# Half of the expert gates added up in a DRAM table by 128 indexed transfers, the other half still by one-hot products

## The chip, the cores and the metric

One core of one Trainium2 chip. The metric is device time in microseconds (us) of the whole program. The engines are TensorE (PE, matrix products), VectorE (DVE), ScalarE (ACT), GpSimd (POOL) and SyncE (SP, which issues most transfers).

## The reference, cut to what matters

The program is a decoder trunk of two layers over 256 tokens of width 1024. Each layer has a mixer, a cross-attention and an expert stage (PEER), and the change is in the last one:

```python
sc = jnp.einsum('thpc,hpkc->thpk', q, sub_keys)       # 8 heads, 2 sides, 128 keys
sv, si = lax.top_k(sc, TOPK)                          # 16 best keys of each side
cand = (sv[..., 0, :, None] + sv[..., 1, None, :])    # 256 sums
fv, fi = lax.top_k(cand, TOPK)                        # 16 best sums
eid = jnp.take_along_axis(cid, fi, axis=-1)           # expert = row key * 128 + column key
g = jax.nn.softmax(fv, axis=-1)
a = jax.nn.gelu(jnp.einsum('thkd,td->thk', ue, xb))
return jnp.einsum('thk,thkd->td', g * a, ve)
```

So each token chooses 16 experts of 16384 in each of 8 heads. The kernel does not gather them. It multiplies all 128 slabs of `u_experts` (a slab is 128 experts by 1024) with all tokens, takes the gelu, multiplies by a dense table of gates that is zero wherever a token has not chosen an expert, and multiplies the result with all 128 slabs of `v_experts`. An expert that a token has chosen in several heads gets the sum of its gates.

## The kernel before

**Slabs.** Weights come as slabs of 512 KB through a ring of `RING` = 4 buffers `raw`. A slab is loaded by SP (`next_slab`, as soon as its buffer is free), ScalarE rounds it to `w_hi` when TensorE has finished the slab that was in the same place (`half_of`, L721 to L725), VectorE makes `w_lo` as the rest (`lo_part`, L848), and TensorE multiplies with `w_hi` and `w_lo`. VectorE's `lo_part` is also what frees the `raw` buffer for the load of the slab four further on.

**The U stage** has 128 slabs. `wide_product` does a slab as 8 pairs of products (L1332 with 512 columns, L1333 with 256). For each slab ScalarE copies half of the result to one of two `h_out` slots, VectorE adds the other half (L1102), ScalarE takes the gelu (L731), and SP stores it to `h_park` in DRAM (L371, 128 KB). `half_of` waits for the store of two slabs before, which frees its slot.

**The choice** lies on VectorE, beside slabs 4 to 71 of U. After the scores of both blocks of 128 tokens come 32 selections of 16 out of 128, 16 of 16 out of 88, and a decoding of the positions to row and column keys (`pick`, L1187 to L1195) for both blocks together. VectorE's order is written out by hand: each piece of the choice calls `spend` with an estimated duration, and for every `LO_EVERY` = 1.56 us spent `next_lo` puts in the `add_u` and `lo_part` of one slab. ScalarE computes the exponentials of both blocks in one instruction after slab `EXP_AT` (L753). Before slab `RET_AT` = 70 TensorE waits for `decoded` and transposes rows, columns and gates of both blocks, six products of 128 columns.

**The gate table** `gate` is [128 columns, 128 rows, 256 tokens] in SBUF, 128 KB in each partition. It is built beside the slabs `HOT_AT` = 72 to 123: for each group of 4 tokens VectorE makes one-hot matrices (`hot_rows`), TensorE does 8 products of 128 columns (`gates_of`, L1690), and ScalarE copies the result (`gate_out`, L761). There are 64 groups, placed in pairs, one pair for every 13 of the chunks (eighths of a slab) by `GROUP_AT`. The slabs 124 to 127 follow without groups (L1326).

**The V stage**: SP loads `h_park` slab by slab, GpSimd multiplies it with `gate` (`gated`, L524), ScalarE and VectorE split it into high and low part (L781, L1253), and TensorE does 12 products of 512 columns (L1715). GpSimd has nothing to do in the U stage. Its list is a wait for `act_ready`, then for the last `hot_row_ready`, then a load of `par`, then the wait for `gate_copied`, then `gated`.

The temporaries of the choice lie in the memory of `gate`, all above 64 KB. `h_out` and the one-hot tiles lie in the memory of `xT`, which is stored to `x_park` before.

## Time and profile before

| | |
|---|---|
| Time, median of 3 runs | 2064.01 us (2063.68 to 2064.97) |
| Profiled execution | 2065.03 us, its span 2063.3 us |
| Granted TensorE clock | 0.999 |
| TensorE busy | 2042.0 us, 99% |
| VectorE, ScalarE, GpSimd busy | 1648.9, 1190.2 and 346.2 us |
| Moved by DMA | 435.54 MB, mean 211 GB/s |

The span is the time from the first to the last instruction of the profiled execution. Layer 0 runs from 0 to about 1020 us of it and layer 1 repeats it 1020.4 us later. In layer 0 the U stage begins at about 289 us and ends at 681 us, and the V stage ends at 1025 us.

### The profile page before, as it was taken

The numbers are of one execution on the slowest core, as the hardware profiler recorded it, in microseconds if no ns is written. First come the engines' busy times: TensorE is split into PE (matmuls) and PEld (weight loads), VectorE is DVE, ScalarE is ACT, GpSimd is POOL, SyncE is SP. The second block draws the span as 40 slices with busy tenths as digits, with TensorE's granted clock in tenths as the row PEclk, the third lists the DMA queues.
The fourth block names the chain that finished last, engine by engine and source line by source line (L and its number), as shares of the span: only waits on it lengthen the run. The fifth ranks groups of instructions, "written<-read, shape, count | busy, mean of one in ns | idle before, by whom it ended". The sixth has DMA issues, their size and how long they took to land.

```text
span 2063.3 us, 38390 instructions
## 1 busy us (share of the span) xinstructions
PE 2042.0 (99%) x11552; PEld 1757.6 (85%) x11552; DVE 1648.9 (80%) x3041; ACT 1190.2 (58%) x1901; POOL 346.2 (17%) x348
## 2 busy tenths in 40 slices
PE   8999999999999999999999999999999999999998
PEld 6888888888888888888888888888888898888886
DVE  7786769999998667676688858799999987676776
ACT  6545556667666555555565545566666665545554
POOL 4010110000000333333340101000000004333331
PEclk9999999999999999999999999999999999999999
DMA  6445457776656877777653554577665567777773
GB/s 222 149 161 169 162 201 236 235 232 209 205 193 199 266 243 240 262 241 241 209 191 127 187 178 164 193 235 239 219 222 196 197 218 255 241 241 262 240 240 126
DMA packets 174249, 435.54 MB, mean 211 GB/s; under 512 B 19504, under 2 KB 85040, under 8 KB 173136
## 3 DMA queue, kind: packets, MB, share of 16 engines
q1 hardware_dynamic: 173520, 430.06, 63.6%
q0 software_dynamic: 640, 4.32, 0.6%
q8 instruction: 53, 0.87, 0.2%
q14 instruction: 36, 0.29, 0.1%
HBM read 397.60 MB, written 36.70 MB: 210 GB/s over the span
## 4 chain that ended last, share of the span: by engine, by line
PE 90%; DVE 6%; ACT 2%; DMA 1%; issue 1%; POOL 0%; SPq 0%; ACTq 0%; DVEq 0%
PE ps L1715 33%; PE ps L1332 30%; PE ps L1333 15%; PE ps L1690 3%; DVE w_lo L848 2%; PE ps L1606 2%; PE ps L1326 2%; PE ps L1737 1%; ACT w_hi L725 1%; PE ps L1631 1%; PE ps L1665 1%; DMA h_park<-h_out 1%; PE ps L1588 1%; DVE pick L1187 1%; DMA raw<-slabs 0%
## 5 line engine op out<-in xcount | busy, mean ns | idle before, releaser
L848 DVE TENSOR_TENSOR w_lo<-raw,w_hi 128x1024 fp32r<-128x1024 f32 x674 | 836.3, 1241 | 264.1 <-ACT w_hi L793 189.5
L1332 PE MATMUL ps<-act,w_hi 128*128 128x512 f32 x2784 | 985.7, 397 | 0.0
L1333 PE MATMUL ps<-act,w_lo 128*128 128x256 f32 x2784 | 777.5, 279 | 0.0
L1332 PEld LDWEIGHTS ps<-act,w_hi 128*128 128x128 f32 x2784 | 521.7, 187 | 114.1 <-issue 0.4
L1715 PE MATMUL ps<-w_hi,act 128*128 128x512 f32 x1936 | 596.4, 389 | 0.0
L1333 PEld LDWEIGHTS ps<-act,w_lo 128*128 128x128 f32 x2784 | 525.5, 189 | 0.3
L793 ACT ACTIVATE w_hi<-raw 128x1024 fp32r<-128x1024 f32 x248 | 263.1, 1061 | 325.2 <-PE ps L1715 325.2
L1715 PEld LDWEIGHTS ps<-w_hi,act 128*128 128x128 f32 x1936 | 363.4, 188 | 75.7
L1715 PE MATMUL ps<-w_lo,act 128*128 128x512 f32 x968 | 376.6, 389 | 0.0
L524 POOL TENSOR_TENSOR h_in<-h_in,gate 128x256 f32<-128x256 f32 x250 | 242.5, 971 | 437.9 <-DMA h_in<-h_park 437.8
L725 ACT ACTIVATE w_hi<-raw 128x1024 fp32r<-128x1024 f32 x248 | 261.1, 1053 | 0.0
L1715 PEld LDWEIGHTS ps<-w_lo,act 128*128 128x128 f32 x968 | 181.7, 188 | 37.5
L552 ACT ACTIVATE w_hi<-raw 128x1024 fp32r<-128x1024 f32 x168 | 177.2, 1055 | 43.7 <-PE ps L1333 26.7
L1253 DVE TENSOR_TENSOR act<-h_in,act 128x256 fp32r<-128x256 f32 x250 | 192.3, 769 | 7.0 <-ACT act L781 7.0
L731 ACT ACTIVATE h_out<-h_out 128x256 f32<-128x256 f32 x248 | 103.3, 416 | 123.6 <-DVE h_out L1102 121.9
L721 ACT ACTIVATE h_out<-ps 128x256 f32<-128x256 f32 x248 | 94.6, 382 | 121.4 <-PE ps L1333 103.7
L516 POOL DMA_DIRECT2D par<-params x2 | 1.2, 593 | 784.5 <-DVE hot_row L1231 784.5
L1102 DVE TENSOR_TENSOR h_out<-h_out,ps 128x256 f32<-128x256 f32 x248 | 102.5, 413 | 16.0 <-ACT h_out L721 15.7
L781 ACT ACTIVATE act<-h_in 128x256 fp32r<-128x256 f32 x250 | 100.0, 400 | 10.1 <-POOL h_in L524 10.1
L1231 DVE TENSOR_TENSOR hot_row<-row_is,g_parts 128x512 f16<-128x512 f16 x256 | 96.7, 420 | 0.0
L1332 PE MATMUL ps<-pre,w_hi 128*128 128x512 f32 x224 | 79.6, 399 | 0.0
L761 ACT ACTIVATE gate<-ps 128x512 f32<-128x512 f32 x128 | 70.4, 591 | 6.1 <-PE ps L1690 6.1
(264 smaller groups left out, 1830.7 us busy)
## 6 DMA issues: line engine op xcount, KB each, us to landing
raw<-slabs SPq DMA_DIRECT2D x680, 512.0 KB, 4.2
h_park<-h_out SPq DMA_DIRECT2D x256, 128.0 KB, 2.3
h_in<-h_park SPq DMA_DIRECT2D x250, 128.0 KB, 3.9
memT<-mem POOLq DMA_DIRECT2D x2, 1024.0 KB, 7.7
skT<-sub_keys POOLq DMA_DIRECT2D x2, 1024.0 KB, 7.4
x_park<-xT SPq DMA_DIRECT2D x2, 1024.0 KB, 6.0
xT<-x_park SPq DMA_DIRECT2D x2, 1024.0 KB, 6.9
xT<-x SPq DMA_DIRECT2D x4, 256.0 KB, 6.2
```

Of the source, the lines that this page charges most:

```text
L524: nc.gpsimd.tensor_tensor(h[:, n:n + 1, :], h[:, n:n + 1, :], gate[:, ds(g * RING + j, 1), :], ALU.mult).then_inc(gated_ready, 1)
L552: nc.scalar.activation(w_hi[:, j].rearrange("p k c -> p (k c)"), raw[:, j, :], ACT.Copy).then_inc(hi_ready, 1)
L725: nc.scalar.activation(w_hi[:, j].rearrange("p k c -> p (k c)"), raw[:, j, :], ACT.Copy).then_inc(hi_ready, 1)
L731: nc.scalar.activation(slot, slot, ACT.Gelu).then_inc(act_evac, 1)
L781: nc.scalar.activation(hi[:, j:j + 1, :], h[:, j:j + 1, :], ACT.Copy).then_inc(ga_hi_ready, 1)
L793: nc.scalar.activation(w_hi[:, j].rearrange("p k c -> p (k c)"), raw[:, j, :], ACT.Copy).then_inc(hi_ready, 1)
L848: nc.vector.tensor_tensor(w_lo[:, j].rearrange("p k c -> p (k c)"), raw[:, j, :], w_hi[:, j].rearrange("p k c -> p (k c)").bitcast(FP32), ...
L1102: nc.vector.tensor_tensor(slot, slot, ps[:, n % RING:n % RING + 1, 0:T], ALU.add).then_inc(u_sum, 1)
L1253: nc.vector.tensor_tensor(lo[:, j:j + 1, :], h[:, j:j + 1, :], hi[:, j:j + 1, :].bitcast(FP32), ALU.subtract).then_inc(ga_ready, 1)
L1332: nc.tensor.matmul(ps[:, j, :], w_hi[:, j, k, :], a[:, :, k, :], start=(k == 0), stop=False)
L1333: return nc.tensor.matmul(ps[:, j, hi * T:hi * T + T], w_lo[:, j, k, :], a[:, hi, k, :], start=False, stop=(k == KB - 1))
L1715: last = nc.tensor.matmul(ps[:, 2 * b + half, :], a[:, j, b * P:(b + 1) * P], w[:, j, 4 * half:4 * half + 4, :].rearrange("p k c -> p (k c)"),
```

## The change

Tokens 0 to 127 (block 0) leave the one-hot way. A table `g_spread` of 8 MB in DRAM is laid out as [128 columns, 128 rows, 128 tokens]. In each layer GpSimd fills it with zeros by four transfers of 2 MB, waits for VectorE's `place_ready`, and issues 128 indexed transfers, one for each head and rank. Each adds 128 single values (one for each token) into the table at the places in `place_u`. After the 16 of a head it waits until all have landed. Then it loads the table back into `gate[:, 0]` by four transfers of 2 MB. Before the first `gated` it waits for them (`spread_back`).

The choice is done block by block: VectorE selects, decodes and normalises block 0 completely, then block 1. There are two exponentials, after slabs 32 and 68. The one-hot way serves tokens 128 to 255 only: 32 groups, in slabs 76 to 123, three transposes before slab 74. `gate` is now [128, 2, 128, 128], and the multiply in `gated` has a fourth dimension.

```diff
-GROUPS = T // 4
-HOT_AT = 72
-RET_AT = 70
-EXP_AT = 60
+GROUPS = P // 4
+HOT_AT = 76
+RET_AT = 74
+EXP_ATS = (32, 68)
...
 EARLY = RING - 1
 H_SLOTS = 2
 HOTS = 2
...
+        place_f = tmp("place_f", 0, [P, PH * TOPK])
+        place_u = tmp("place_u", 0.5, [P, PH * TOPK], U32)
+        g_flat = tmp("g_flat", 1, [P, PH * TOPK])
+        zeros = tmp("zeros", 40, [P, ZERO_ROWS, P])
+
+        g_spread = nc.dram_tensor("g_spread", (P * NKEYS * P, 1), FP32, kind="Internal").ap()
...
+            spread = g_spread.rearrange("(p n t) o -> p n (t o)", p=P, n=NKEYS)
...
+                nc.gpsimd.memset(zeros[:], 0.0).then_inc(zeros_set, 1)
+                pool.wait_ge(zeros_set, layer + 1)
+                for n in range(0, NKEYS, ZERO_ROWS):
+                    pool.dma_start(spread[:, n:n + ZERO_ROWS, :], zeros[:]).then_inc(zeroed, 16)
+                pool.wait_ge(zeroed, (layer + 1) * (NKEYS // ZERO_ROWS * 16))
+                pool.wait_ge(place_ready, layer * 2 + 2)
+                for h in range(PH):
+                    for i in range(h * TOPK, (h + 1) * TOPK):
+                        nc.gpsimd.indirect_dma_start(g_spread, bass.IndirectOffsetOnAxis(ap=place_u[:, i:i + 1], axis=0),
+                                                     g_flat[:, i:i + 1], None, compute_op=ALU.add).then_inc(scattered, 16)
+
+                    pool.wait_ge(scattered, (layer * PH + h + 1) * (TOPK * 16))
+                for n in range(0, NKEYS, ZERO_ROWS):
+                    pool.dma_start(gate[:, 0, n:n + ZERO_ROWS, :], spread[:, n:n + ZERO_ROWS, :]).then_inc(spread_back, 16)
+
                 pool.wait_ge(hot_row_ready, (layer + 1) * GROUPS + 1)
                 settle(pool)
                 pool.dma_start(par[:], params[ds(layer + 1, 1)].rearrange("o p f -> (o p) f")).then_inc(par_loaded, 16)
                 pool.wait_ge(gate_copied, (layer + 1) * GROUPS + RING)
                 settle(pool)
+                pool.wait_ge(spread_back, (layer + 1) * (NKEYS // ZERO_ROWS * 16))
+                settle(pool)
 
                 def gated(g, j, h, n):
 
                     pool.wait_ge(h_loaded[j], (layer * (V_SLABS // RING) + g) * 16 + 16)
                     settle(pool)
-                    nc.gpsimd.tensor_tensor(h[:, n:n + 1, :], h[:, n:n + 1, :], gate[:, ds(g * RING + j, 1), :],
+                    of_h = h[:, n, :].rearrange("p (b o t) -> p b o t", b=TB, o=1)
+                    nc.gpsimd.tensor_tensor(of_h, of_h, gate[:, :, ds(g * RING + j, 1), :],
                                             ALU.mult).then_inc(gated_ready, 1)
 
...
-                nc.scalar.activation(g_exp[:], g_exp[:], ACT.Exp).then_inc(gexp_ready, 1)
-                experts(EXP_AT, HOT_AT - RING - EXP_AT)
+                at = RING
+                for b, exp_at in enumerate(EXP_ATS):
+                    experts(at, exp_at - at)
+                    act.wait_ge(fin_ready, layer * TB + b + 1)
+                    chosen = g_exp[:, b * PH:(b + 1) * PH, :]
+                    nc.scalar.activation(chosen, chosen, ACT.Exp).then_inc(gexp_ready, 1)
+                    at = exp_at
+                experts(at, HOT_AT - RING - at)
...
-                    nc.scalar.activation(gate[:, :, 4 * n:4 * n + 4],
+                    nc.scalar.activation(gate[:, 1, :, 4 * n:4 * n + 4],
...
-                for n in range(0, TB * SETS, 2):
-                    if n % SETS == 0:
-                        dve.wait_ge(sc_evac, layer * TB + n // SETS + 1)
-                        settle(dve)
-                    src = (scores0, scores1)[n // SETS]
+                for b, src in enumerate((scores0, scores1)):
+                    dve.wait_ge(sc_evac, layer * TB + b + 1)
+                    settle(dve)
+                    for n in range(b * SETS, (b + 1) * SETS, 2):
+                        step.join()
+                        top16(*[(src[:, m % SETS, :], struck[:, m - n, 0:NKEYS], top_v[:, m, :], top_u[:, m, :])
+                                for m in (n, n + 1)], us=0.29)
                     step.join()
-                    top16(*[(src[:, m % SETS, :], struck[:, m - n, 0:NKEYS], top_v[:, m, :], top_u[:, m, :])
-                            for m in (n, n + 1)], us=0.29)
-                step.mark(nc.vector.tensor_copy(top_i[:], top_u[:]))
-
-                step.join()
-                for b in range(TB):
+                    step.mark(nc.vector.tensor_copy(top_i[:, b * SETS:(b + 1) * SETS, :], top_u[:, b * SETS:(b + 1) * SETS, :]))
...
+                    cs = slice(b * PH, (b + 1) * PH)
+                    flat = slice(b * PH * TOPK, (b + 1) * PH * TOPK)
+                    nc.vector.tensor_tensor(g_exp[:, cs], fin_v[:, cs], fin_v[:, cs, 0:1].to_broadcast([P, PH, TOPK]),
+                                            ALU.subtract).then_inc(fin_ready, 1)
+                    flat_i = fin_i[:, cs].rearrange("p c k -> p (c k)")
+                    step.mark(nc.vector.tensor_scalar(bit_u[:, flat], flat_i, 8, None, ALU.bitwise_and))
...
+                    spend(1.0)
...
+                        for a in range(TOPK):
+                            step.mark(nc.vector.scalar_tensor_tensor(
+                                pick[:, a, cs], place[:, flat].rearrange("p (c k) -> p c k", k=TOPK), float(a),
+                                keys[:, :, side, a].unsqueeze(2).to_broadcast([P, PH, TOPK]), ALU.is_equal, ALU.mult))
+                            spend(0.26)
+                        n = TOPK // 2
+                        while n:
+                            step.join()
+                            out = (found[:, flat].rearrange("p (o c k) -> p o c k", o=1, k=TOPK) if n == 1
+                                   else pick[:, 0:n, cs])
+                            step.mark(nc.vector.tensor_tensor(out, pick[:, 0:n, cs], pick[:, n:2 * n, cs], ALU.add))
+                            spend(0.07 * n + 0.2)
+                            n //= 2
+                    step.join()
+                    if b == 0:
+                        step.mark(nc.vector.scalar_tensor_tensor(place_f[:], col_f[:, flat], float(NKEYS), row_f[:, flat],
+                                                                 ALU.mult, ALU.add))
+                    dve.wait_ge(gexp_ready, layer * TB + b + 1)
+                    step.link(nc.vector.tensor_reduce(g_sum[:, cs], g_exp[:, cs], AX.X, ALU.add))
+                    step.link(nc.vector.reciprocal(g_sum[:, cs], g_sum[:, cs]))
+                    of_sum = g_sum[:, cs].unsqueeze(2).to_broadcast([P, PH, TOPK])
+                    if b == 0:
+                        dve.wait_ge(consts, 5)
+                        nc.vector.tensor_scalar(place_u[:], place_f[:], float(P), tok[:, 0:1], ALU.mult, ALU.add).then_inc(place_ready, 1)
+                        nc.vector.tensor_tensor(g_flat[:].rearrange("p (c k) -> p c k", k=TOPK), g_exp[:, cs], of_sum,
+                                                ALU.mult).then_inc(place_ready, 1)
+                    else:
+                        nc.vector.scalar_tensor_tensor(g_exp[:, cs], g_exp[:, cs], GATE_SCALE, of_sum,
+                                                       ALU.mult, ALU.mult).then_inc(decoded, 1)
                 while due[0] < HOT_AT + 1:
                     next_lo()
                 dve.wait_ge(ret_mm, layer + 1)
-                step.mark(nc.vector.tensor_copy(pick_at[:].rearrange("p i n e -> p (i n e)"), ps[:, 4, :]))
-                g_pairs = ps[:, 5, 0:T].rearrange("p (n e) -> p n e", e=2)
+                step.mark(nc.vector.tensor_copy(pick_at[:].rearrange("p i n e -> p (i n e)"), ps[:, 4, 0:T]))
+                g_pairs = ps[:, 4, T:T + P].rearrange("p (n e) -> p n e", e=2)
...
-                    for b in range(TB):
-                        last = nc.tensor.transpose(ps[:, 4 + i // 2, (i % 2) * T + b * P:(i % 2) * T + (b + 1) * P],
-                                                   src[:, b * P:(b + 1) * P], ident[:])
+                    last = nc.tensor.transpose(ps[:, 4, i * P:(i + 1) * P], src[:, P:2 * P], ident[:])
```

## Rows read from the trace of the kernel before

**Rows 1.** The page: busy time of each engine, its share and instructions.

```profile
PE 2042.0 (99%) x11552; PEld 1757.6 (85%) x11552; DVE 1648.9 (80%) x3041; ACT 1190.2 (58%) x1901; POOL 346.2 (17%) x348
```

**Rows 2.** Windows of layer 0: length, busy time of each engine, clock, DMA share, GB/s.

```profile
365.00:385.00 20.00, 20.00 (x117) 17.62 (x117) 19.39 (x70) 12.73 (x23) 0.00 (x0) 1.00 0.71 238
...
445.00:465.00 20.00, 20.00 (x117) 17.64 (x116) 17.99 (x34) 13.57 (x23) 0.00 (x0) 1.00 0.77 240
...
485.00:505.00 20.00, 19.75 (x136) 17.18 (x135) 18.66 (x40) 11.48 (x22) 0.00 (x0) 1.00 0.71 217
```

**Rows 3.** The chain in order of time: start, length, what.

```profile
197.28 1.75 PE ps L1619 x16
...
529.08 0.93 PE ps L1690 x16
534.58 0.93 PE ps L1690 x16
...
681.16 337.31 PE ps L1715 x1488
```

**Rows 4.** Timeline of TensorE, first and last of 48 wide products: start, length.

```profile
433.93 0.39 PE L1332 MATMUL ps<-act,w_hi 128*128 128x512 f32 x1
...
450.23 0.39 PE L1332 MATMUL ps<-act,w_hi 128*128 128x512 f32 x1
```

**Rows 5.** Timeline of VectorE in the first choice: one slab's two operations and what follows.

```profile
340.98 0.40 DVE L1102 TENSOR_TENSOR h_out<-h_out,ps 128x256 f32<-128x256 f32 x1
341.31 1.23 DVE L848 TENSOR_TENSOR w_lo<-raw,w_hi 128x1024 fp32r<-128x1024 f32 x1
342.45 0.48 DVE L1115 MAX8 top_v<-scores 128x8 f32<-128x128 f32 x2
```

**Rows 6.** Timeline of VectorE: end of the second choice, then three of the pick operations.

```profile
437.75 0.42 DVE L1161 TENSOR_TENSOR g_exp<-fin_v 128x256 f32<-128x256 f32 x1
...
445.63 1.09 DVE L1187 SCALAR_TENSOR_TENSOR pick<-a_at,top_i 128x256 bf16<-128x256 bf16 x3
446.63 0.41 DVE L1102 TENSOR_TENSOR h_out<-h_out,ps 128x256 f32<-128x256 f32 x1
```

**Rows 7.** Groups of instructions over the whole run.

```profile
L1124 DVE MAX8 top_v<-struck 128x8 f32<-128x128 f32 x64 | 15.4, 284 | 0.1
...
L1124 DVE MAX8 fin_v<-struck 128x8 f32<-128x88 f32 x32 | 6.4, 243 | 0.1
```

**Rows 8.** Timeline of ScalarE at the one exponential of a layer.

```profile
461.67 1.28 ACT L753 ACT_TABLE_LOAD   x1
...
463.40 1.28 ACT L721 ACT_TABLE_LOAD   x1
...
466.04 1.28 ACT L731 ACT_TABLE_LOAD   x1
```

**Rows 9.** Timeline of GpSimd at the start of the value stage.

```profile
665.45 0.59 POOL L516 DMA_DIRECT2D par<-params  x1 [392.23 <-DVE hot_row L1231]
672.37 3.41 POOL L524 TENSOR_TENSOR early_in<-early_in,gate 128x256 f32<-128x256 f32 x3 [6.33 <-DMA early_in<-h_park]
```

**Rows 10.** The page: DMA issues, KB each, us from issue to landing.

```profile
h_park<-h_out SPq DMA_DIRECT2D x256, 128.0 KB, 2.3
```

**Rows 11.** DMA queues (packets, MB, share) during GpSimd's memT load: 24-26, then 1047-1048 us.

```profile
q0 software_dynamic: 81, 0.66, 82.1%
q1 hardware_dynamic: 27, 0.11, 13.4%
...
q0 software_dynamic: 37, 0.30, 72.0%
q1 hardware_dynamic: 25, 0.10, 25.4%
```

**Rows 12.** DMA from 530 to 660 us: totals, then issues with us to landing.

```profile
DMA packets 11099, 25.60 MB, mean 197 GB/s; under 512 B 1231, under 2 KB 6095, under 8 KB 11087
...
raw<-slabs SPq DMA_DIRECT2D x38, 512.0 KB, 3.5
```

76 lines of the change are left out of this document (28 added, 48 removed).

## The prediction

> **What bounds the kernel now.** The page's busy times come first: TensorE is busy for 2042.0 of 2063.3 us, VectorE for 80% of the span [rows 1]. The windows of layer 0 then show whether that holds beside the work that is changed. In the choice TensorE has 20.00 of 20 us and VectorE 19.39. Only the window before the one-hot groups has a hole, of 0.25 us [rows 2]. The chain of waits in order of time runs through the groups of one-hot products in a steady beat of one pair every 5.50 us, and the V stage is one piece of 337 us [rows 3]. So the reader is to see that TensorE sets the time, that what leaves its list is gained in full, and that VectorE is close behind. GpSimd is free in the whole U stage, but its queue feeds the same DMA engines as SP's, which carry 197 GB/s there [rows 12].
>
> The sum is made against the profiled execution, 2065.03 us. That is 1.0 above the median of the three timed runs. Two per mille of the time, 4.1 us, is about what a measurement can tell from no change.
>
> **TensorE.** 48 wide products took 16.30 us from the first to the last start, 47 steps of 0.3468 [rows 4], so a slab takes 2.774 us. A pair of groups comes every 5.50 us with 13 chunks, 4.51 us, around it [rows 3]. The rest, 0.99 us, is the pair, 0.495 for a group. Its 16 products alone are 0.93, which is the lower bound (0.465). There are 32 groups fewer in each of two layers: 64 × 0.495 = 31.7 us (29.8 by the lower bound). Three transposes in a layer go too. 16 of the attention's took 1.75 us [rows 3], so six are 0.7 us. Together −32.4 us, for 2032.6 if nothing else moves. Slabs 72 to 75 only change from having groups beside them to having none.
>
> **VectorE.** One slab's two operations take 1.47 us of its list (340.98 to 342.45, [rows 5]). The four slabs more before HOT_AT bring 4 × 2.774 of time and take 4 × 1.47, so 5.2 us are added for the choice. The added cost is 42 decoding operations done in halves. A pick of 256 elements takes 0.334 us (three in 1.00, [rows 6]). One of 128 is not in the trace. It lies between half of that (no cost) and the whole of it (+14 us a layer). Between 128 and 88 elements MAX8 goes from 284 to 243 ns [rows 7], about 1 ns an element, which makes a half pick 0.20 us and the 42 pairs 2.9 us dearer. Some six new small operations add about 1.3. That is 4.2 of 5.2 us, so nothing. At the upper bound 10 us would be missing, about the idle time that VectorE has left over the choice (5% of 200 us, [rows 2]), so at most a few us.
>
> The waits for the exponentials keep their place. The list before has 81.0 us of `spend` up to `fin_ready`, 52 slabs put in, so VectorE is at 56, which needs slab 52's product, and it was there at 437.75 [rows 6]. After the change the first `fin_ready` has 40.5 (26 slabs, VectorE at 30), ahead of ScalarE's place at 32. The block's decoding ends at 54.9 (35 slabs, place 39), behind it. For the second block the places are 65 and 74, against 68, and TensorE asks for it before slab 74 where it now asks before 70 with VectorE ending at 71. The 0.25 us may stay or go. ScalarE pays three table loads and one exponential more, 3 × 1.28 + 0.3 = 4.1 us [rows 8], once at slab 32. TensorE had 20.00 of 20 us around the present one [rows 2], since `w_hi` is made three slabs ahead. I cost it at nothing. Without that cover it is 4.1 less ScalarE's idle time, some 3 us a layer.
>
> **GpSimd's list.** `place_ready` comes 16.7 slabs (81.0 − 54.9 over 1.56) before 437.75, at 391.4, with the tail of the block at about 393 us. The V stage begins at 681.16 [rows 3], 16 earlier after the change, 665. Its first multiply (1.14 of 3.41 us, [rows 9]) and the two splits need about 2.5 us before, so the table must be back by 662.5. That leaves 269 us for eight times 16 indexed transfers, eight landings, and the read back. A small transfer lands in 2.3 us [rows 10], eight of them 18. The read back is 8.39 MB: GpSimd's queue moved 0.66 MB in 2 us and 0.30 in 1 [rows 11], so 25 to 28 us and a landing. What remains is 269 − 18 − 29 = 222, and 1.7 us for each of 128 transfers. None is in the trace. Below, a direct transfer with one run for each partition costs GpSimd 0.59 us [rows 9]; an indexed one cannot be cheaper, as it also reads its places. Above, it costs its landing, 2.3 us. I take the middle, 1.45, as it has the shape of the first and work that the first has not. It fits, 32 us early.
>
> **The four large transfers in a layer** share the DMA engines with SP's. While GpSimd loaded 1 MB of `memT`, SP's queue moved only 27 packets (0.11 MB) in 2 us beside 81 of the other, and 25 (0.10 MB) in 1 us at another time [rows 11]: 55 to 100 GB/s where the U stage asks for 197 [rows 12]. Over 25 to 28 us the slabs come 14 to 18 us late. The cover is what lies ahead in the ring. A slab lands 3.5 us after its issue [rows 12], issued when the slab eight before is done and split, so it can be 6 us early for `w_hi`, and the split weights another 6.6 us early for TensorE; with VectorE taking them in its listed order it is less. I take 9 to 12.6 us. The read back then stalls TensorE for 1 to 9 us, and I take 5 in each layer, +10. The zeros go out at about 281 us, beside two blocks of score products in which TensorE uses no slab for 7 us, so 14 to 18 late become 7 to 11, inside the cover: 0, at most 2.
>
> **Sum:** 2065.0 − 32.4 + 10 = **2042.6 us**.
>
> **The rivals.**
>
> *The indexed transfers end too late* (the other side). The V stage waits for `spread_back`, and each 0.1 us of pace above 1.7 costs 2 × 12.8 = 26 us. It decides from 1.79, where the 22.4 us are gone. At a pace of 2.0 it is 77 us, 2119; at 2.3 it is 154, 2196. For it: 128 places must be read and each value read, added and written, and the middle of my bounds is only 0.25 from the limit. Against: GpSimd has nothing else, and 16 may be in flight. VectorE, 19.39 of 20 us busy [rows 2], may also hold GpSimd up. The worst form is that no two of the 128 overlap, each costing its landing of 2.3 us: 294 us against 269 − 29 = 240, so 54 late a layer, 2151. Chance 0.29 for the whole rival, 0.08 of it for this form.
>
> The Trainium skill ("DMA: Bandwidth & Descriptors", Anatomy of one DMA) states for that form a fixed cost of about 2.0 us for each transfer that GpSimd issues, mostly the wait for completion. By that figure the sum would be an estimated 256 us against the 240, and 2075 us; the landing of 2.3 us agrees with it, and no row has two small transfers of GpSimd in flight.
>
> *The covers hold and nothing stalls*: 2032.6. For it: ring and score products absorb whole loads elsewhere at 20.00 of 20 us. Against: [rows 11]. Chance 0.21.
>
> *The large transfers take it all back*, so that the change does not do what it says: SP's queue stands still for 25 to 28 us at each read back, less 9 of cover, 16 to 19 a layer, 32 to 38 in all, 2065 to 2071. For it: a run of the table is 16 KB where `memT` had 8, and `h_park`'s stores, which free ScalarE's slots, are as late as the loads. Chance 0.10.
>
> *The single values crowd the DMA engines or GpSimd slows VectorE* during slabs 36 to 110. An engine 5% short for 200 us costs 10 us a layer, 20 in all, with the rest 2063; twice that, 2083. Nothing in the rows gives its size. Chance 0.06.
>
> My forecast, 2034 to 2058, has 0.34. **Chances:** faster 0.21 + 0.34 + 0.03 of the last two = 0.58; within 4.1 us 0.07 (most of the third rival); slower 0.29 + 0.06 = 0.35. The range goes from 2031, all hidden, to 2125, which takes in the late transfers up to a pace of 2.0 and leaves out about 0.15.
>
> **What would show it.** Half as many L1690 products, pairs 24 chunks apart, and TensorE at 20.00 of 20 us through slabs 4 to 75. In GpSimd's rows the time from one indexed transfer to the next: under 1.7, and `spread_back` landed well before the V stage, or a hole in TensorE at its start. In the windows of the read back, SP's queue at a quarter of its rate and a hole of some 5 us in TensorE some 10 us later; no hole at the zeros. The prediction is wrong if the pace is above 1.7, or if `raw` and `h_park` land later during the whole of the indexed transfers and not only beside the large ones.

## The result and the profile after

The changed kernel takes 2177.8 us, median of four runs (2172.1 to 2180.5), beside 2064.5 for the kernel before (2063.7 to 2065.4). The ratio is 1.0539 [1.0526, 1.0553]: 113 us slower, where 22 us faster was forecast. The profiled execution has a span of 2175.8 us, 112.5 over that of before.

The page, its engine row, answers to [rows 1]. TensorE's busy time is 10.7 us less and its share has fallen from 99% to 93%. GpSimd has gone from 346 to 835 us.

```profile
PE 2031.3 (93%) x11034; PEld 1735.5 (80%) x11034; DVE 1583.1 (73%) x2899; ACT 1201.4 (55%) x1873; POOL 835.0 (38%) x623
```

Two groups of instructions over the whole run (line, engine, operation, count, busy us and mean ns, then idle us before them and what ended it) tell where the time is:

```profile
L536 POOL DMA_INDIRECT g_spread<-g_flat,place_u x256 | 475.7, 1858 | 385.7 <-DVE g_flat L1246 249.5 <-issue 89.7 <-DMA g_spread<-g_flat,place_u 46.5
...
L1759 PE MATMUL ps<-w_hi,early_hi 128*128 128x512 f32 x24 | 10.9, 454 | 109.3 <-issue 109.3
```

TensorE stands idle for 109.3 us ahead of the first products of the V stage, over the two layers. That is the loss but for 3 us, because the gain of the groups was lost again, as the chain shows. The chain of waits of layer 0, in order of time (start, length, what), answers to [rows 3]:

```profile
282.08 23.95 DMA raw<-slabs
...
669.35 11.51 PE ps L1372 x96
680.86 52.27 issue
733.13 26.98 PE ps L1759 x111
```

The same chain in the trace of before, at the tail of the U stage:

```profile
669.66 11.51 PE ps L1326 x96
```

The reader is to see three things. The U stage ends as late as before (its tail began at 669.66 then, at 669.35 now), although 32 groups were taken out, so the gain of some 16 us was lost again within it. Then comes a hole of 52.27 us. And early in U one load of raw weights holds the chain for 23.95 us. GpSimd's timeline says what the hole waited for:

```profile
403.31 1.66 POOL L536 DMA_INDIRECT g_spread<-g_flat,place_u  x1 [124.83 <-DVE g_flat L1246]
...
705.76 1.55 POOL L536 DMA_INDIRECT g_spread<-g_flat,place_u  x1 [0.30 <-issue]
709.01 2.20 POOL L541 DMA_DIRECT2D gate<-g_spread  x4 [1.70 <-DMA g_spread<-g_flat,place_u]
...
731.34 2.27 POOL L556 TENSOR_TENSOR early_in<-early_in,gate 128x256 f32<-128x256 f32 x3 [19.60 <-DMA gate<-g_spread]
```

The 128 transfers take from 403.31 to 705.76, 2.38 us from one to the next. The last has landed at 709.0, the read back takes 22.3 more, and GpSimd's first multiplication starts 1.8 us ahead of TensorE's 733.13. The windows of TensorE (length, busy time, granted clock, DMA share, GB/s) answer to [rows 2]:

```profile
280.00:300.00 20.00, 20.00 (x129) 1.00 1.03 433
300.00:320.00 20.00, 17.53 (x103) 0.91 0.71 255
...
680.00:700.00 20.00, 0.86 (x8) 0.62 0.20 1
700.00:720.00 20.00, 0.00 (x0) 0.50 0.59 201
720.00:740.00 20.00, 6.87 (x24) 0.60 0.80 308
```

At 280 to 300 us the zeros fill all 16 DMA engines. TensorE pays some 10 us later, with 2.5 us of hole and a clock of 0.91 (before, it was busy for 20.00 of 20 us there at 1.00). In the hole at 700 the clock is granted at its lower level (0.50, 1.2 GHz), and it is still 0.60 in the window in which V begins; from 740 us to the end of V it is 1.00 again and TensorE is never idle.

### The profile page after: what moved, and what is told of

Its sections match the earlier page's. It is cut to its first block, busy times and chain, and to the rows that moved or that the text cites. A ratio compares the mean times of both kernels' runs of the same rounds, so it can differ in the third digit from the quotient of the medians.

```text
span 2175.8 us, 37411 instructions
## 1 busy us (share of the span) xinstructions
PE 2031.3 (93%) x11034; PEld 1735.5 (80%) x11034; DVE 1583.1 (73%) x2899; ACT 1201.4 (55%) x1873; POOL 835.0 (38%) x623
## 4 chain that ended last, share of the span: by engine, by line
PE 62%; DVE 11%; POOL 11%; DMA 7%; issue 6%; ACT 3%; SPq 0%; ACTq 0%; DVEq 0%; POOLq 0%
PE ps L1759 31%; PE ps L1378 16%; POOL g_spread L536 10%; PE ps L1379 8%; DVE w_lo L884 5%; DMA raw<-slabs 3%; DMA g_spread<-g_flat,place_u 2%; PE ps L1652 2%; DMA h_park<-h_out 1%; ACT w_hi L757 1%; DVE h_out L1138 1%; PE ps L1372 1%; DMA gate<-g_spread 1%; PE ps L1781 1%; PE ps L1677 1%
## 5 line engine op out<-in xcount | busy, mean ns | idle before, releaser
L1378 PE MATMUL ps<-act,w_hi 128*128 128x512 f32 x2784 | 997.3, 402 | 11.1 <-DVE w_lo L884 5.8
L536 POOL DMA_INDIRECT g_spread<-g_flat,place_u x256 | 475.7, 1858 | 385.7 <-DVE g_flat L1246 249.5
L1299 DVE TENSOR_TENSOR act<-h_in,act 128x256 fp32r<-128x256 f32 x250 | 202.6, 810 | 9.4 <-ACT act L817 9.4
L1759 PE MATMUL ps<-w_hi,early_hi 128*128 128x512 f32 x24 | 10.9, 454 | 109.3 <-issue 109.3
L1759 PEld LDWEIGHTS ps<-w_hi,early_hi 128*128 128x128 f32 x24 | 5.2, 216 | 111.2 <-issue 109.7
```

The source lines that it names most:

```text
L536: nc.gpsimd.indirect_dma_start(g_spread, bass.IndirectOffsetOnAxis(ap=place_u[:, i:i + 1], axis=0), g_flat[:, i:i + 1], None, compute_op=A ...
L1299: nc.vector.tensor_tensor(lo[:, j:j + 1, :], h[:, j:j + 1, :], hi[:, j:j + 1, :].bitcast(FP32), ALU.subtract).then_inc(ga_ready, 1)
L1378: nc.tensor.matmul(ps[:, j, :], w_hi[:, j, k, :], a[:, :, k, :], start=(k == 0), stop=False)
L1759: last = nc.tensor.matmul(ps[:, 2 * b + half, :], a[:, j, b * P:(b + 1) * P], w[:, j, 4 * half:4 * half + 4, :].rearrange("p k c -> p (k c)"),
```

## The experiments

Each time is a median beside the kernel before on the same chip (2064.0 to 2067.0 us there). In all diffs the lines are those of the changed kernel.

### Taking the table apart

**No table.** The zeros, the indexed transfers and the read back go, and GpSimd sets the gates of block 0 to zero.

```diff
-for n in range(0, NKEYS, ZERO_ROWS):
-    pool.dma_start(spread[:, n:n + ZERO_ROWS, :], zeros[:]).then_inc(zeroed, 16)
...
-for h in range(PH):
-    for i in range(h * TOPK, (h + 1) * TOPK):
-        nc.gpsimd.indirect_dma_start(g_spread, bass.IndirectOffsetOnAxis(ap=place_u[:, i:i + 1], axis=0),
-                                     g_flat[:, i:i + 1], None, compute_op=ALU.add).then_inc(scattered, 16)
-    pool.wait_ge(scattered, (layer * PH + h + 1) * (TOPK * 16))
-for n in range(0, NKEYS, ZERO_ROWS):
-    pool.dma_start(gate[:, 0, n:n + ZERO_ROWS, :], spread[:, n:n + ZERO_ROWS, :]).then_inc(spread_back, 16)
+nc.gpsimd.memset(gate[:, 0, 3:], 0.0).then_inc(zeros_set, 1)
+nc.gpsimd.memset(gate[:, 0, 0:3], 0.0).then_inc(zeros_set, 1)
```

> The kernel after without the DRAM table: no zeros, no indexed transfers, no read back (the gates of tokens 0 to 127 are set to zero by GpSimd instead, so that part of the result is left out). The choice block by block and the 32 one-hot groups of tokens 128 to 255 stay. Theory A (GpSimd's row of 256 indexed transfers with their waits ends too late for the V stage, and the rest of the loss is transfers that the U stage's loads stand behind): the 52 and 57 us in front of the V stage go, and nearly all of the 32 us that the 64 removed groups gave comes to light: 2033 to 2042 us. Rival B (the choice in two halves, with TensorE's slower step of 0.353 us in the loops of U, costs by itself what the groups gave): 2050 to 2065 us.

2050.0 us, 0.9914 [0.9897, 0.9930]. Theory A had 2033 to 2042, so half of what the groups give is missing with no table at all. That is just in the range of rival B. This became the question of the second part.

**No indexed transfers, no bulk, half of the heads.** In the first only the loop over the heads of the diff above is taken out. In the second the two loops around it are out and it stays. In the third it runs over heads 0 to 3:

```diff
-for h in range(PH):
+for h in range(PH // 2):
```

> The kernel after without its 128 indexed transfers a layer; zeros and read back stay (the gates of tokens 0 to 127 are zero). Theory A: 109 us of waiting in front of the V stages go, the delay by the zeros (about 24 us in which the loads of raw weights land late, of which TensorE loses some 6 a layer) stays: 2045 to 2060 us, 8 to 16 above the kernel without a table. Rival C (the 16384 single values of a head block crowd the DMA engines, and the zeros do nothing): the same as the kernel without a table within 3 us. Rival D (the bulk transfers, and not the indexed ones, hold the V stage): above 2100 us.

> The kernel after with its indexed transfers, but no zeros written before them and no read back after them (the gates of tokens 0 to 127 are zero, the table is added to and never read). Theory A: the indexed transfers still end at about 707 us of the span in layer 0, which is some 25 us after the V stage could start, and the 22 to 24 us of the read back in each layer and the 6 to 8 of the zeros go: 2177.8 - 46 - 14 = 2118 us, range 2108 to 2130. Rival D (the bulk transfers hold everything up): 2035 to 2070 us.

> The kernel after with the indexed transfers of four heads of eight (64 a layer; the gates of the other four heads of tokens 0 to 127 are left out). Theory A: 64 x 2.37 = 152 us, so that they end near 555 us in layer 0 and the read back is done before the V stage; no wait in front of it: 2177.8 - 109 = 2069 us less what the U stage gets back, 2055 to 2069 us. If the price of one transfer rises because fewer of them have to be out at once or because the read back itself is what is late, it stays above 2090.

Without indexed transfers 2093.3 us, 1.0124 [1.0107, 1.0141], 43 above the kernel without a table. The 8 to 16 of theory A were far too few, and neither rival's time (2050, above 2100) was met. The windows of both, no table first, show where:

```profile
400.00:460.00 60.00, 59.59 (x335) 1.00 0.73 224
```

```profile
400.00:460.00 60.00, 45.28 (x229) 0.89 0.82 298
```

The read back falls in the middle of the U stage here, and TensorE loses 14.3 us to it in that window. Without the bulk transfers 2123.0 us, 1.0268 [1.0245, 1.0291], as A said (2118). Its chain has this hole before V:

```profile
674.12 32.93 issue
```

V begins at 707.0. The last indexed transfer is issued at 700.4, the last has landed at 703.4, and the first multiplication and the splits fill the rest. So the two parts cost 43 and 73 us over the 2050 and 116 of 128 together. With half of the heads 2098.4 us, 1.0148 [1.0131, 1.0165]: the hole before V is gone, but the time is above A's 2055 to 2069. The read back is now issued at 557 us, inside the U stage, and costs there much of what it costs in the kernel without indexed transfers (2093): from 520 to 640 us TensorE is busy for 99.7 us of 120, where it is 118.5 without a table.

### Where the gain of the groups went

**The choice in halves alone.** One-hot products for all 256 tokens (64 groups, gates and transposes as before), the choice block by block, exponentials at 32 and 68, no table. Of its edit only the first lines are shown; the rest puts the tiles and the gates of both blocks back as they were.

```diff
-GROUPS = P // 4
+GROUPS = T // 4
```

> The kernel after with the choice block by block and its places in the U stage (exponentials at slabs 32 and 68, transposes at 74, first one-hot rows at 76), but with no table at all: the gates of all 256 tokens come from one-hot products, 64 groups a layer as before. This is the choice block by block alone. Theory A (the handover from the choice to the one-hot rows is late by some 4.6 us a layer, and TensorE's step in the U loops is 0.353 instead of 0.347 us in part of them, some 4 us a layer): 9 to 18 us slower than before, 2073 to 2083 us. Rival (the choice in halves costs nothing and what the kernel without a table lost comes from something else in it): 2061 to 2068 us.

2081.4 us, 1.0079 [1.0063, 1.0096]: the choice in halves, with its places in U, costs 17 us by itself. That is A's number; its reasons did not stand, as the next runs show.

**Later rows.** The kernel without a table, its second exponential four slabs earlier and its transposes and one-hot rows four slabs later.

```diff
-HOT_AT = 76
-RET_AT = 74
-EXP_ATS = (32, 68)
+HOT_AT = 80
+RET_AT = 78
+EXP_ATS = (32, 64)
```

> The kernel without the table (2050 us), with its second exponential four slabs earlier (64) and the transposes and the first one-hot rows four slabs later (78 and 80). Theory A: VectorE is no longer late with the one-hot rows (2.9 us a layer) and ScalarE's three tables are loaded where nobody waits (1.7 us a layer): 2050 - 2 x 4.6 = 2041 us, 2037 to 2045. Rival (the step of TensorE is what was lost): 2048 to 2052 us.

2049.6 us, 0.9931 [0.9914, 0.9947], against 2050.0: nothing. Theory A's reason, a handover placed too early, fell. The rival's number is met, but not its reason (TensorE's longer step), as the last section shows. ScalarE's timeline of the kernel without a table (start, length, line) has loads of its function tables where no exponential is near:

```profile
410.61 1.28 ACT L742 ACT_TABLE_LOAD   x1
...
413.26 1.28 ACT L752 ACT_TABLE_LOAD   x1
```

One such pair comes in every pass of four slabs, from 398.8 to 482.4. The groups over the whole run, in the kernel without a table and in that of the next experiment:

```profile
L742 ACT ACT_TABLE_LOAD x22 | 28.2, 1283 | 0.6 <-DMA h_park<-h_out 0.2
```

```profile
L742 ACT ACT_TABLE_LOAD x6 | 7.7, 1283 | 0.1
```

In the kernel before there are six as well. Its own timeline has the sign of it, 9 us behind the last line of [rows 8]: its loop after the exponential has two passes, and the second loads the pair again.

```profile
474.85 1.28 ACT L721 ACT_TABLE_LOAD   x1
...
477.49 1.28 ACT L731 ACT_TABLE_LOAD   x1
```

A loop that is entered with the exponential's table and ends with gelu's has its loads inside its body, at the first copy and the first gelu, and pays them in each pass. Before, that loop had 2 passes. The changed kernel put an exponential at slab 32, and the loop behind it has 9. The Trainium skill ("ScalarE activation tables: per-element evaluation and per-set limits", Table sets in the compiler and the runtime) says that the compiler's back end places the table loads per block. The counts of 22 and 6 agree with that, if the body of a loop is such a block.

**The first pass written out.**

```diff
 nc.scalar.activation(chosen, chosen, ACT.Exp).then_inc(gexp_ready, 1)
-at = exp_at
+first = RING if b == 0 else 0
+if first:
+    experts(exp_at, first)
+at = exp_at + first
```

> The kernel without the table (2050 us). Its trace shows ScalarE loading a table of 1.28 us twice in each pass of the loop of four slabs that stands between the two exponentials (pairs at 398.82 and 401.47, 410.61 and 413.26, and so on to 482.44); before the first exponential there are none. Here the first pass after the first exponential is written out ahead of the loop, so that the loop is entered with the tables that it ends with. Theory E (these loads make ScalarE late with w_hi, after it VectorE with w_lo and the one-hot rows, and TensorE's short holes bring the step of 0.353 us): 2050 - 10 = 2040 us, 2036 to 2045. Rival (VectorE alone is late, because the choice is cut in halves): 2047 to 2052 us.

> The choice block by block with one-hot products for all 256 tokens and no table (2081 us, 17 above before), with the same pass written out. Theory E (the reloaded tables are what the choice in halves cost): 2081 - 13 = 2068 us, 2064 to 2072. Rival (VectorE's work in halves costs by itself): 2075 to 2082 us.

> The whole kernel after, with only the first pass after the first exponential written out ahead of ScalarE's loop (which gave 13 us in the kernel without a table). Theory A (the V stage starts when the chain on GpSimd is done, whatever the U stage does before): nothing comes of it, 2172 to 2180 us. Rival (what the U stage loses is lost in this kernel too, and the hole in front of the V stage does not cover it): 2160 to 2168 us.

Without a table 2036.9 us, 0.9864 [0.9847, 0.9880], 13.1 less: theory E. With one-hot products for all tokens 2069.0 us, 1.0019 [1.0010, 1.0029], 12.4 less. Each beside the kernel before on its own chip, the halves cost 17.4 us and now 3.5. So nearly all of the 17 us were reloaded tables, and 3.5 are left for the halves. In the whole kernel the same edit gives 2173.7 us, 1.0531 [1.0512, 1.0550], four less, inside A's range and within the spread of its runs. Its chain of waits says why:

```profile
663.17 11.50 PE ps L1375 x96
674.68 56.99 issue
731.67 28.54 PE ps L1762 x114
```

The U stage is 6.2 us shorter than in the changed kernel (669.35) and the hole 4.7 longer (52.27).

### The chain on GpSimd

**VectorE and the indexed transfers.** In the changed kernel many transfers take more than 1.55 us. GpSimd's timeline and, below it, VectorE's in the same stretch:

```profile
457.94 2.27 POOL L536 DMA_INDIRECT g_spread<-g_flat,place_u  x1 [0.31 <-issue]
460.52 2.05 POOL L536 DMA_INDIRECT g_spread<-g_flat,place_u  x1 [0.30 <-issue]
462.87 2.60 POOL L536 DMA_INDIRECT g_spread<-g_flat,place_u  x1 [0.30 <-issue]
```

```profile
457.57 1.23 DVE L884 TENSOR_TENSOR w_lo<-raw,w_hi 128x1024 fp32r<-128x1024 f32 x1
...
459.92 1.22 DVE L884 TENSOR_TENSOR w_lo<-raw,w_hi 128x1024 fp32r<-128x1024 f32 x1
...
462.82 1.23 DVE L884 TENSOR_TENSOR w_lo<-raw,w_hi 128x1024 fp32r<-128x1024 f32 x1
```

The split ends at 458.80, 461.14 and 464.05, that is 0.86, 0.62 and 1.18 us after each transfer's start, and the transfer takes 1.41, 1.43 and 1.42 from there: it seems to begin its work when the split is over. In the whole of layer 0, 51 of the 60 transfers that start during a split last 1.40 to 1.44 us beyond its end. Those 60 hold 36 of the 37.5 us by which the row of 128 exceeds 1.55 each; the 68 others take 1.57 on the mean. From 680 us, when VectorE idles, all take 1.54 to 1.57. In the next kernel the split is made from one input (the low parts of the weights are then wrong):

```diff
-nc.vector.tensor_tensor(w_lo[:, j].rearrange("p k c -> p (k c)"), raw[:, j, :],
-                        w_hi[:, j].rearrange("p k c -> p (k c)").bitcast(FP32),
-                        ALU.subtract).then_inc(lo_ready[j], 1)
+nc.vector.tensor_scalar(w_lo[:, j].rearrange("p k c -> p (k c)"),
+                        w_hi[:, j].rearrange("p k c -> p (k c)").bitcast(FP32),
+                        2.0 ** -12, None, ALU.mult).then_inc(lo_ready[j], 1)
```

> The kernel after with VectorE's split of each raw slab, w_lo, made from one input (w_hi times a constant) in place of two (raw minus w_hi); the low parts of all weights are then wrong. Theory A, that a GpSimd transfer which finds VectorE in an operation with two inputs from SBUF waits for its end: the indexed transfers fall from a mean of 1.84 us to near 1.55, the row of 128 ends some 37 us sooner in each layer, and the V stages start as much sooner: 2178 - 74 = 2104 us, 2095 to 2118. Rival (the longer ones wait for a DMA ring or for memory, and not for VectorE): mean still 1.8 or more, 2165 to 2180 us. Between the two if the operation with one input runs at a double rate and holds the same ports for half as long, which the Trainium skill (SBUF - State Buffer, two separate sides) gives for such operations: mean 1.6 to 1.75, 2120 to 2160 us.

2130.0 us, 1.0310 [1.0293, 1.0327], 48 less, in the case between the two. The groups of the run: the transfers here, then the splits from 420 to 660 us in the changed kernel and here (minimum, median, maximum in ns):

```profile
L536 POOL DMA_INDIRECT g_spread<-g_flat,place_u x256 | 423.2, 1653 | 393.3 <-DVE g_flat L1246 250.0 <-issue 96.6 <-DMA g_spread<-g_flat,place_u 46.8
```

```profile
L884 DVE TENSOR_TENSOR w_lo<-raw,w_hi x80: 1208/1225/1261, 419.3 to 658.6; 128x1024 fp32r<-128x1024 f32 x80
```

```profile
L884 DVE TENSOR_SCALAR w_lo<-w_hi x80: 685/694/1042, 419.3 to 658.3; 128x1024 fp32r<-128x1024 f32 x80
```

An operation 0.69 us long in place of 1.22 takes two thirds of the excess over 1.55 away (0.31 to 0.10 us a transfer), 52.5 us of GpSimd's busy time, and the kernel is 48 us shorter: nearly one to one, as it must be where a chain sets the end. The Trainium skill ("SBUF — State Buffer", SBUF: two separate sides) says that a VectorE operation with two inputs in SBUF, or one in a double-rate mode, and a GpSimd instruction that reads SBUF exclude each other for its whole length. The long splits agree with it; the short ones do so if they run in such a mode, which their length suggests and no run here shows by itself.

**The waits between heads.** Even heads add into one table, odd heads into a second that is not read. A head then waits for the one two before it.

```diff
+table, landed = ((g_spread, scattered), (g_spread_2, scattered_2))[h % 2]
+pool.wait_ge(landed, (layer * (PH // 2) + h // 2) * (TOPK * 16))
```

> The kernel after, with the heads of even number added into one table and those of odd number into a second one that is neither zeroed nor read back (their gates are left out), so that no head has to wait for the landing of the one before it. Theory A (fixed issue time of each transfer, waits for landings, VectorE's operations with two inputs, one after the other): the waits of some 30 us a layer go: 2178 - 60 = 2118 us, 2112 to 2127. Rival (the transfers queue up behind each other once nothing waits for them, and GpSimd is held at the issue): their mean rises over 2.0 us and the time stays above 2140.

> Two tables as in the run beside it and w_lo from one input as in the earlier run that gave 2130 us. Theory A (the parts add up): 2178 - 60 - 48 = 2070 us, 2062 to 2080; the last transfer lands near 650 us in layer 0, the read back before the V stage, and the long hole in front of it is gone, but the kernel is still no faster than before, for the 17 us of the choice in halves and the zeros and the read back remain. Rival (the read back in the last slabs of U costs as much as the hole did): above 2085.

With two tables 2127.7 us, 1.0302 [1.0285, 1.0320], 50 less and just above the range of A (2112 to 2127): in its profiled execution (2120.9 us, the fastest of its four) the V stage starts at 709.3, 24 sooner, not 30. The waits between heads, 29 us, are gone, but the mean transfer rose from 1.84 to 1.89 us, 6 us in all. With w_lo from one input as well 2089.0 us, 1.0116 [1.0099, 1.0133], above A's 2062 to 2080. The long hole is gone, as forecast, but the read back now lies in the last slabs of U, where the chain waits 10.8 and 15.2 us for stores of `h_park` behind it. The rival (above 2085) has it: the parts do not add up, since a burst that leaves the hole meets stores and loads that the U stage needs.

**What one transfer costs.** Transfers of 64 places in place of 128:

```diff
-nc.gpsimd.indirect_dma_start(g_spread, bass.IndirectOffsetOnAxis(ap=place_u[:, i:i + 1], axis=0),
-                             g_flat[:, i:i + 1], None, compute_op=ALU.add).then_inc(scattered, 16)
+nc.gpsimd.indirect_dma_start(g_spread, bass.IndirectOffsetOnAxis(ap=place_u[0:P // 2, i:i + 1], axis=0),
+                             g_flat[0:P // 2, i:i + 1], None, compute_op=ALU.add).then_inc(scattered, 16)
```

and, in a kernel of its own, transfers that write in place of adding:

```diff
-                             g_flat[:, i:i + 1], None, compute_op=ALU.add).then_inc(scattered, 16)
+                             g_flat[:, i:i + 1], None).then_inc(scattered, 16)
```

> The kernel after with its 128 indexed transfers a layer, each of them for the first 64 partitions alone (the gates of tokens 64 to 127 are left out). Theory H (GpSimd works through the places one by one, 12 ns each): 1.55 becomes some 0.8 us, the row of 128 takes some 200 us and is over before the V stage, and the time is near that of the kernel with half of the heads: 2098 us, 2090 to 2108. Rival (the price is of the transfer, whatever it holds): 1.5 us or more each, 2165 to 2180 us.

> The kernel after with its indexed transfers writing the gates over the zeros in place of adding them (where two heads choose the same expert, one gate is lost). Theory A (GpSimd's issue time is what bounds the row, and it does not know what the DMA engine does with the value): 1.55 us stays; the landings are 1 to 2 us shorter, eight times a layer: 2178 - 2 x 8 x 1.5 = 2154 us, 2148 to 2172. Rival (the adding holds the queue back and with it GpSimd): the mean of 1.86 us falls below 1.6 and the time below 2140.

2108.4 us, 1.0212 [1.0195, 1.0229], and 2094.3 us, 1.0156 [1.0137, 1.0175]. The transfers of layer 0 (minimum, median, maximum in ns, first and last start) in the changed kernel, with 64 places each, and copied:

```profile
L536 POOL DMA_INDIRECT g_spread<-g_flat,place_u x128: 1544/1550/3850, 403.3 to 705.8; - x128
```

```profile
L536 POOL DMA_INDIRECT g_spread<-g_flat,place_u x128: 1390/1399/3591, 403.0 to 665.1; - x128
```

```profile
L536 POOL DMA_INDIRECT g_spread<-g_flat,place_u x128: 954/1028/2504, 403.4 to 618.2; - x128
```

Half of the places save 0.15 of 1.55 us: neither the 0.8 of theory H nor quite the fixed price of its rival. From 1.55 and 1.40 one works out, as an estimate from two points, some 1.25 us that do not depend on the places. The time is at the edge of H's range all the same, since the row of 128 starts is 41 us shorter: the mean transfer, with what VectorE adds, fell from 1.84 to 1.62 us, and the landings are shorter too. Writing in place of adding saves 0.6 us of GpSimd's own time (1.84 to 1.21 on the mean). Theory A said that it stays at 1.55 and falls here; the minimum is 0.95 and the time below 2140, on the rival's side. The pages have a sign of why. GpSimd's queue in the changed kernel, with 64 places, and copied (packets, MB, share of 16 engines):

```profile
q0 software_dynamic: 39808, 38.02, 8.4%
```

```profile
q0 software_dynamic: 23424, 37.96, 7.3%
```

```profile
q0 software_dynamic: 11136, 38.02, 4.8%
```

Without indexed transfers it has 2944 packets. So each of the 256 transfers makes 144 packets when it adds to 128 places, 80 for 64 places and 32 when it writes. More packets go with more of GpSimd's time, but not in proportion (64 fewer save 0.15 us, 112 fewer 0.5 to 0.6), so what the rest of the difference is stays open.

**A quarter is enough.** V waits for the first of the four pieces of the read back, and for each other at its slab.

```diff
-pool.wait_ge(spread_back, (layer + 1) * (NKEYS // ZERO_ROWS * 16))
+pool.wait_ge(q_back[0], layer * 16 + 16)
```

> The kernel after, but GpSimd's first multiplication of the V stage waits only for the first of the four pieces of the read back, and for each further piece at the slab that needs it. Theory A (the V stage waits for the end of the whole chain on GpSimd): 22 us from issue to the last landing become 6 to 9: 2178 - 2 x 14 = 2150 us, 2145 to 2160. Rival (four pieces share the DMA engines and land close together, or the V stage then stands behind the pieces' own traffic): 2168 to 2180 us.

2166.6 us, 1.0491 [1.0474, 1.0509]: 11 less, under half of A's 28. The chain of waits from the read back on:

```profile
710.72 7.50 DMA gate<-g_spread
...
718.49 0.73 POOL early_in L558
...
720.02 10.22 DMA h_park<-h_out
...
731.38 7.12 DMA h_in<-h_park
```

The first slab is gated at 718.49, 12.9 us sooner (in an execution of 2172.4 us, the slowest of its four). But the fourth slab's `h_in` cannot be loaded before a store that takes 10.22 us (2.3 in [rows 10]) and then takes 7.12 itself, behind the other three pieces.

### The bulk transfers, and the whole mended

**Small pieces.** Zeros and read back in 16 pieces of eight rows, each issued when the one before has landed, without indexed transfers. Then the same with the first pass of ScalarE's loop written out. Of the edit, the part of the read back:

```diff
+PIECE = 8
+for i, n in enumerate(range(0, NKEYS, PIECE)):
+    pool.dma_start(gate[:, 0, n:n + PIECE, :], spread[:, n:n + PIECE, :]).then_inc(spread_back, 16)
+    pool.wait_ge(spread_back, (layer * (NKEYS // PIECE) + i + 1) * 16)
```

> The kernel without the indexed transfers (2093 us, 43 above the one without a table), with the zeros and the read back in 16 pieces of eight rows (0.5 MB), each issued when the one before has landed, in place of four of 2 MB at once. Theory F (the loads of the raw weights on SyncE's queue stand behind a burst that takes all 16 DMA engines, 433 GB/s in that stretch): the bytes are the same and the burst is not, and most of the 43 us comes back: 2055 to 2065 us. Rival (the bytes cost what they cost, in whatever pieces): 2085 to 2095 us.

> Zeros and read back in 16 pieces of 0.5 MB, no indexed transfers (2079 us), with the same pass written out. Theory G (the pieces made stores and loads land one or two us later, which cost TensorE something only because ScalarE had no reserve left beside its table loads): near the 2037 us of the kernel without table and with that pass, 2039 to 2050 us. Rival (17 MB a layer of extra traffic cost their 29 us in any case): 2062 to 2068 us.

2079.3 us, 1.0064 [1.0047, 1.0081], and 2075.3 us, 1.0051 [1.0033, 1.0070]. Of the 43 us 14 are of the burst; theory F wanted 28 to 38, its rival at most 8. Theory G fell more clearly: with ScalarE's loads gone the pieces still cost 38 us over the 2036.9, which is above its rival's range too (2062 to 2068). The waits of ScalarE from 280 to 720 us (total, times, longest), without a table and with the pieces, both with the pass written out:

```profile
ACT h_out L742 <- DMA h_park<-h_out: 13.5, 16, 1.6
```

```profile
ACT h_out L747 <- DMA h_park<-h_out: 54.7, 47, 3.2
```

From 280 to 480 us a store of `h_park` lands after 3.3 us where it landed after 2.1, and only two slots of `h_out` exist. So ScalarE waits and is late with `w_hi`, VectorE with `w_lo`, and TensorE in turn: it is busy for 54.25 of 60 us from 400 to 460. Of the chain that ended last, the page gives 8% to these stores, and 1% without a table, again with the pass written out. Beside the zeros, before VectorE's choice of block 1, the same lateness cost TensorE nothing (20.00 of 20 us in each window from 280 to 380). More slots for `h_out` were not tried.

**Mended.** The whole kernel with that pass written out, zeros in 16 pieces, and a read back of 16 pieces, two out at a time, each taken by V at its slab.

> The whole kernel after, with that pass written out, the zeros in 16 pieces one after the other, and the read back in 16 pieces of eight rows of which two are out at a time, the V stage waiting for the first of them and taking each further one at the slab that needs it. Theory A: the transfers still end at about 707 us in layer 0 (1.85 us each at the least, and the waits), the first piece is there 5 instead of 22 us later and the loads of h do not stand behind a burst: 2178 - 2 x 15 = 2148 us, 2138 to 2155; above the kernel before in any case. Rival (as with the quarters, half of it is lost again in front of the fourth slab): 2160 to 2170 us.

2138.3 us, 1.0356 [1.0339, 1.0373], 39 less than the changed kernel and in A's range. GpSimd's timeline:

```profile
704.56 1.55 POOL L538 DMA_INDIRECT g_spread<-g_flat,place_u  x1 [0.30 <-issue]
707.91 1.18 POOL L543 DMA_DIRECT2D gate<-g_spread  x2 [1.79 <-DMA g_spread<-g_flat,place_u]
...
713.10 2.10 POOL L560 TENSOR_TENSOR early_in<-early_in,gate 128x256 f32<-128x256 f32 x3
```

From the read back's issue to the first multiplication it is 5.2 us instead of 22.3. The transfers still end where they did: the last has landed at 707.9, 33 us after TensorE could begin (674.9). No version of the table, not even one with gates left out, came below the kernel before.

## Why the prediction was wrong

The step that failed is the pace of the indexed transfers, taken as 1.45 us with a limit of 1.7. The first rival, that the transfers end too late, had a chance of 0.29 and is what happened. It is also the first sign that the prediction named for its being wrong, a pace above 1.7.

- *Pace.* From the timeline of layer 0, the row took 709.01 − 403.31 = 305.7 us where the prediction had 1.45 × 128 + 18 = 204, and GpSimd was idle for 70.0 of them. A transfer keeps GpSimd for 1.55 us when nothing disturbs it, 1.84 on the mean, and 0.30 follow each. The fixed part alone, 1.85, is above the limit. VectorE's splits add 0.29 (the run with one input took two thirds of it away). The eight landings add 32 us, 4.0 each where the prediction had 2.3; the run with two tables showed most of that. The middle between 0.59 and 2.3 was chosen for want of a row; the direct transfer's 0.59 was no near relation. The mapping from pace to time was right: the prediction gave 2196 for a pace of 2.3 with its landings apart. Here pace and gap are 2.14 and the extra landing time 14 us a layer, 2.25 with it spread over the 128: some 2042.6 + 26 × 5.5 = 2186 by the prediction's own price, against 2178. That it comes so near is partly luck: a start 10 us later, a read back 7 us shorter and a stall of +10 that does not fall due beside a hole nearly cancel.
- *The form of rival 1 in which no two transfers overlap* had 294 us for the row, near the 305.7, but is not what was seen: the 16 of a head follow each other at 1.85 us and more, and only the last one's landing is waited for. The same rival had named VectorE as what may hold GpSimd up, and that was seen.
- *Start and read back.* 403 in place of 393; the exponential of block 0 was at 389.67 in the changed kernel and at 383.66 without a table, so 6 of the 10 us come from the zeros' delay (without bulk transfers the first indexed one starts at 396.96). The read back took 22.3 us against 27 to 30: right, a little dear.
- *TensorE, −32.4 us.* Right. The kernel with neither the DRAM table nor reloaded function tables is 28.6 faster than before, and the halves cost 3.5. The two kernels with that pass written out differ by these groups: 2069.0 − 2036.9 = 32.1.
- *VectorE, nothing.* 3.5 us, in the bounds.
- *ScalarE's second exponential, nothing, "without that cover some 3 us a layer".* Wrong, 6 us a layer, and for a reason that was not in the sum: not the three loads at the exponential but two in each of nine passes behind it. The window around the present exponential (20.00 of 20 us) was read as cover; the timeline one pass further held the pair at 474.85.
- *Large transfers, +10 and nothing for the zeros.* Too small. In the whole kernel the read back lies in the hole and costs its full 22 us a layer; where it lies in U, a burst costs 14.3 in one window instead of 5. The zeros, costed at 0 to 2, cost 2.5 us of hole and a stretch at a clock of 0.91.
- *The last rival, single values crowding or GpSimd slowing VectorE.* It was the other way round, VectorE slows GpSimd: its splits take 1.225 us beside the indexed transfers and 1.221 without a table (460 to 520 us). Nor did the single values cost TensorE much: with indexed but without bulk transfers the tail of U begins at 662.61, without a table at 662.99. With the pass written out they may cost some 3 us a layer (116.8 of 120 us busy from 460 to 580 in the whole kernel, 120.0 without a table), which no run parts from the zeros' delay.

How the 113 us are made up, by the runs: −32 for the groups, +3.5 for the halves, +12.5 for the reloaded function tables, +43 for the bulk transfers, +73 for the indexed ones, and 12 that only the two together cost, 112 in all. These are not independent. In the whole kernel the 12.5 are hidden in the hole (4 came back, within the spread), and the bulk transfers lie in another place than in the run that prices them.

## What to carry to other kernels

A row of small dependent operations is costed as the product of its count and the whole price of one (busy, gap, the landings, and what holds the engine up), and an operation that no trace shows is bounded by its worst end where the limit lies inside the bounds: here the limit was 1.7 between 0.59 and 2.3, and that was the risk of the whole change. When a function of another table moves ahead of a loop, count the table loads in the loop's passes, and write the first pass out. A transfer that uses free DMA bandwidth is not free: it makes its neighbours land later, so ask first which small ring of buffers (here the two slots of `h_out`) waits for such a landing.

## What was not expected of the hardware

- Adding in place of writing costs GpSimd 0.6 us for each indexed transfer (1.55 against 0.95), and 64 places less only 0.15. The adding one makes 144 packets, the writing one 32.
- TensorE's step in the U loops is one of two. In the kernel without a table the wide products start at

```profile
410.73 0.39 PE L1367 MATMUL ps<-act,w_hi 128*128 128x512 f32 x1
...
414.55 0.39 PE L1367 MATMUL ps<-act,w_hi 128*128 128x512 f32 x1
415.02 0.50 PE L1367 MATMUL ps<-act,w_hi 128*128 128x512 f32 x1
415.48 0.40 PE L1367 MATMUL ps<-act,w_hi 128*128 128x512 f32 x1
...
419.37 0.40 PE L1367 MATMUL ps<-act,w_hi 128*128 128x512 f32 x1
```

  11 steps of 0.347 us (as in [rows 4]), a hole of some 0.2 us, and then 11 of 0.354, at the same granted clock. It stays so over many slabs. In the changed kernel it is so from 313 to 409 us: TensorE is busy for 60.00 of 60 us from 340 to 400 in both, with 349 products before and 341 after. That is about 1.9% of a loop, an estimated 5 us in a U stage (from its some 100 slabs of 2.774 us). The step changed in these traces only where the row of products was interrupted, by a hole or by other products. It does not explain the 13 us of ScalarE's loads: the kernel without a table and with the pass written out, the fastest of all, has 0.353 from 302 us on, behind the score products and with no hole. Why, no run shows.
